# The gate and up products of both feed-forward layers by a seven-product scheme, two of its four weight sums added by an accumulating DMA

## What is computed

```python
def swiglu_ffn(h, w_gate, w_up, w_down):
    return (jax.nn.silu(h @ w_gate) * (h @ w_up)) @ w_down

def reference(...):
    ...
    for i in range(DEPTH):          # DEPTH = 2
        h = rms_norm(h_res, ln_mix[i])
        mix = s5_mixer(...) if i % 2 == 0 else sink_window_attention(...)
        h_res = h_res + mix
        h_res = h_res + swiglu_ffn(rms_norm(h_res, ln_ffn[i]),
                                   ffn_w_gate[i], ffn_w_up[i], ffn_w_down[i])
    return rms_norm(h_res, ln_f)[:, N_META:]
```

## Time and profile before

| | |
|---|---|
| three executions | 1181.73, 1182.28, 1182.97 us; median 1182.28 us |
| span of the profiled execution, first to last instruction | 1177.9 us (no separate time is given for it; the runs are 4.4 us above it) |
| PE busy | 1140.4 us, 97% of the span |
| DVE busy | 553.8 us, 47% |
| ACT busy | 412.4 us, 35% |
| POOL busy | 174.8 us, 15% |
| moved by DMA | 104.63 MB, mean 89 GB/s |

### The profile page before, as it was taken

The page is one execution under the profiler, slowest core; times in us unless marked ns, Lnnn a source line. Parts: engine busy times, 40 slices in busy tenths (PEclk is TensorE's granted clock), DMA queues, the critical chain, the costliest instruction groups (busy, mean ns, idle before and its releaser), DMA issues.

```text
span 1177.9 us, 20443 instructions
## 1 busy us (share of the span) xinstructions
PE 1140.4 (97%) x8362; PEld 1025.8 (87%) x8362; DVE 553.8 (47%) x845; ACT 412.4 (35%) x701; POOL 174.8 (15%) x114
## 2 busy tenths in 40 slices
PE   5799999999999999999999899989999999999998
PEld 5688899999999999999999676678888888888887
DVE  7978444443344333444334355455443434434444
ACT  6823232332222222233323455443322223223332
POOL 4699000011111111100000000001111111110000
PEclk9999899999999999999999999999999999999999
DMA  7164333222323232222323211022333233223332
GB/s 141 24 163 111 87 109 108 72 89 91 98 80 100 78 107 71 76 83 91 98 81 126 72 37 42 32 72 72 108 107 99 79 107 107 75 73 97 98 98 94
DMA packets 119387, 104.63 MB, mean 89 GB/s; under 512 B 21868, under 2 KB 117216, under 8 KB 119008
## 3 DMA queue, kind: packets, MB, share of 16 engines
q1 hardware_dynamic: 110120, 99.85, 27.9%
q10 hardware_dynamic: 9216, 4.06, 1.5%
HBM read 98.11 MB, written 5.24 MB: 88 GB/s over the span
## 4 chain that ended last, share of the span: by engine, by line
PE 90%; DVE 4%; DMA 2%; ACT 1%; POOL 1%; issue 1%; SPq 0%; ACTq 0%; DVEq 0%; POOLq 0%
PE banks L1380 79%; PE banks L1520 1%; PE banks L1457 1%; PE banks L1510 1%; PE banks L1731 1%; PE banks L1734 1%; PE banks L1752 1%; PE banks L1721 1%; PE banks L1458 1%; DMA y_dram<-y_act 1%; PE banks L1746 1%; PE banks L1472 0%; POOL col_mag L499 0%; PE banks L1720 0%; ACTq L719 0%
## 5 line engine op out<-in xcount | busy, mean ns | idle before, releaser
L587 ACT CAST w_high<-raw 128x1024 fp32r<-128x1024 f32 x186 | 195.0, 1049 | 572.1 <-PE banks L1380 572.1
L945 DVE TENSOR_TENSOR w_low<-raw,w_high 128x1024 fp32r<-128x1024 f32 x186 | 228.2, 1228 | 208.3 <-ACT w_high L587 208.3
L1380 PE MATMUL banks<-x_high,w_high 128*128 128x512 f32 (+2 forms) x1184 | 321.0, 324 | 1.0 <-DVE x_low L1173 1.0
L1380 PE MATMUL banks<-x_high,w_low 128*128 128x512 f32 (+2 forms) x1184 | 318.5, 322 | 0.0
L1380 PE MATMUL banks<-x_low,w_high 128*128 128x512 f32 (+2 forms) x1184 | 317.7, 321 | 0.0
L1380 PEld LDWEIGHTS banks<-x_high,w_high 128*128 128x128 f32 x1184 | 198.9, 189 | 19.4 <-issue 2.2
L1380 PEld LDWEIGHTS banks<-x_low,w_high 128*128 128x128 f32 x1184 | 198.9, 188 | 16.1
L1380 PEld LDWEIGHTS banks<-x_high,w_low 128*128 128x128 f32 x1184 | 198.2, 188 | 16.8
L1380 PE MATMUL banks<-a_high,w_high 128*128 128x256 f32 (+2 forms) x533 | 141.2, 318 | 0.0
L1380 PE MATMUL banks<-a_low,w_high 128*128 128x256 f32 (+2 forms) x533 | 141.1, 318 | 0.0
L1380 PE MATMUL banks<-a_high,w_low 128*128 128x256 f32 (+2 forms) x533 | 141.1, 318 | 0.0
(11 more groups left out here) (288 smaller groups left out, 1249.3 us busy)
## 6 DMA issues: line engine op xcount, KB each, us to landing
raw<-in_ffn_w_gate SPq DMA_DIRECT2D x22, 1024.0 KB, 5.3
raw<-in_ffn_w_up SPq DMA_DIRECT2D x22, 1024.0 KB, 5.3
raw<-in_ffn_w_down SPq DMA_DIRECT2D x16, 768.0 KB, 4.4
raw<-in_ffn_w_down SPq DMA_DIRECT2D x16, 640.0 KB, 4.1
raw<-in_attn_w_qkv SPq DMA_DIRECT2D x6, 1024.0 KB, 5.0
k_toep<-k_dram SPq DMA_DIRECT2D x64, 64.0 KB, 2.6
raw<-in_ssm_w_glu_b SPq DMA_DIRECT2D x4, 1024.0 KB, 5.5
raw<-in_ssm_w_glu_a SPq DMA_DIRECT2D x4, 1024.0 KB, 5.8
```

What stands on the lines that cost most here:

```text
L587: nc.scalar.copy(high[:, j], raw[:, slot, :, j * P:(j + 1) * P]).then_inc(w_rounded, 1)
L945: nc.vector.tensor_tensor(low[:, j], raw[:, slot, :, j * P:(j + 1) * P], high[:, j], ALU.subtract).then_inc(w_split, 1)
L1380: ins = nc.tensor.matmul(banks[:, bank + h, b0:b0 + cn], w[:, j, k, :], xx[:, first_k + k, c0 + base:c0 + base + cn], start=start and k == ...
```

## The change

The gate tile and the up tile of 256 columns become one "unit" each. A unit's weights are cut into blocks: input features in even and odd blocks of 128 (4 pairs, `KP`), columns in two halves. The tokens are cut into two halves too (264 or 256). The four quarter outputs, which took eight products of quarters, come from seven products with sums of quarters (the form with 15 additions). Four of the additions are on the weights, four on the input (made once a layer, `x_t`, and kept as slots T1 to T4 of `xs_high`/`xs_low` beside the three plain ones), seven on the outputs.

The weight sums: `raw` has five block columns now. SP loads the even rows into blocks 0 and 1, the odd rows into 3 and 4, and the odd rows' second half once more into block 2 (256 KB). When the three have landed, POOL issues a DMA that adds the even rows from HBM onto blocks 1 and 2 (512 KB, `add_sums`). DVE makes the other two sums, `sum2` and `sum4`. All seven forms of a unit's weights are rounded by ACT and split by DVE.

The outputs: three intermediate sums are copied from PSUM by ACT (`copied_part`), three quarter outputs are added or subtracted by DVE, the fourth is read from its bank. `silu` of both gate blocks is one instruction. The factor `rstd_row` is no longer put on the gated activations by POOL; the results of the down products are multiplied by it on DVE (`scale_down`). The down product is done in three stages, after 4, 8 and 11 pairs of units, over 3, 4 and 4 pairs of feature blocks, each added onto the residual. POOL's descriptor area is 4096 bytes. The loops of ACT and DVE over the feed-forward are written out.

```diff
-DOWN_TILES = ((0, 6), (6, 6), (12, 5), (17, 5))
+KP = KB // 2
+STAGES = ((0, 3), (3, 7), (7, 11))
+UPS = ((0, 4), (4, 8), (8, 11))
+UNITS = 2 * N_UP + N_DOWN * len(STAGES)
+TOK = HALF
+Y_BANK, W_BANK, X_BANK = (0, 4), (1, 5), (2, 6)
+B11, B21, B22, T1, T2, T3, T4 = range(7)
...
+            def load_unit(layer, unit, src):
+                g, kp = UNITS * layer + unit, pairs_of(unit)
...
+                    sp.wait_ge(t_split, forms_before(g - 1))
+                w, blocks = src.rearrange("p (k i) n -> p k i n", i=2), blocks_of(g, kp)
+                for i in range(2):
+                    sp.dma_start(blocks[:, :, 3 * i:3 * i + 2, :].rearrange("p k o c -> p k (o c)"), w[:, :, i, :]).then_inc(unit_loaded[g % 2], 16)
+                if is_up(unit):
+                    sp.dma_start(blocks[:, :, 2, :], w[:, :, 1, P:]).then_inc(unit_loaded[g % 2], 16)
...
-                        nc.gpsimd.tensor_tensor(gate[:, j, a:e], gate[:, j, a:e], rstd_row[:, a:e], ALU.mult).then_inc(gate_scaled, 1)
+            def add_sums(layer, i, w):
...
+                pool.wait_ge(unit_loaded[g % 2], 16 * loads_before(g + 2))
+                nc.gpsimd.dma_start(blocks_of(g, KP)[:, :, 1:3, :].rearrange("p k o c -> p k (o c)"), rows_even,
+                                    accum_op=ALU.add).then_inc(sums_landed[g % 2], 16)
...
+                def gate_unit(i, behind):
+                    g, kp = UNITS * layer + up_unit(i), KP
+                    copy_first(g)
+                    round_column(g + 1, kp)
+                    copy_sum(g)
+                    round_s2(g + 1, kp)
+                    if behind:
+                        round_acts(i - 1)
+                    copy_last(g)
+                    round_sums(g + 1, kp)
...
+                    round_corner(g + 1, kp)
+                    round_s4(g + 1, kp)
...
+            def sum2(g, kp):
+                dve.wait_ge(sums_landed[g % 2], 16 * (ups_before(g) // 2 + 1))
+                if g > 0:
+                    dve.wait_ge(t_split, forms_before(g))
+                    dve.wait_ge(s4_made, ups_before(g))
+                w = blocks_of(g, kp)
+                TT(s24[:, 0, 0:kp], w[:, :, 0, :], w[:, :, 2, :], ALU.add).then_inc(s2_made, 1)
...
+                def gate_unit(i, behind):
...
+                    sum2(g + 1, kp)
+                    sum4(g + 1, kp)
...
+                    first_corner(g, gate_part(n, 0, 0))
...
+                    split_column(g + 1, kp)
+                    if behind:
+                        split_acts(i - 1)
+                    split_s2(g + 1, kp)
+                    last_corner(g, gate_part(n, 1, 1))
...
+                    split_sums(g + 1, kp)
+                    low_corner(g, gate_part(n, 1, 0))
...
+                    TT(gate_part(n, 0, 1), bank_part(Y_BANK[g % 2], n), rstd_part(n, 1), ALU.mult).then_inc(set_free, 1)
...
+                    split_corner(g + 1, kp)
+                    split_s4(g + 1, kp)
...
+            def part(w, i, x, slots, c, bank, n, start=False, need=None):
+                for m, slot in enumerate(slots):
+                    if need is not None:
+                        need(m)
+                    for a, b in ((0, 0), (0, 1), (1, 0)):
+                        ins = nc.tensor.matmul(bank_part(bank, n), w[a][:, m, i, :], x[b][:, slot, c, :],
...
+                ins.then_inc(part_done, 1)
+            def summed_unit(g, ups, downs, parity, x, n, first=False, spread_at=None, mean_at=None, need_b11=None, need_all=None):
...
+                pe.wait_ge(t_split, forms + (4 if first else 1))
+                part(col, 0, x, slots, B11, y, n, start=True, need=need_b11)
+                if spread_at is not None:
+                    spread(spread_at, n)
+                part(col, 1, x, slots, B21, v, n, start=True, need=need_all)
+                pe.wait_ge(t_split, forms + (4 if first else 2))
+                pe.wait_ge(part_copied, 3 * ups + 1)
+                part(w2, 0, x, slots, T2, y, n)
+                if mean_at is not None:
+                    mean(mean_at, n)
+                pe.wait_ge(t_split, forms + (5 if first else 3))
+                part(sums, 0, x, slots, T3, w, n, start=True)
+                pe.wait_ge(part_copied, 3 * ups + 2)
+                part(sums, 1, x, slots, T1, y, n)
+                pe.wait_ge(t_split, forms + (5 if first else 4))
+                pe.wait_ge(part_copied, 3 * ups + 3)
+                part(w2, 1, x, slots, T4, w, n)
+                pe.wait_ge(t_split, forms + 5)
+                pe.wait_ge(c22_made, ups + 1)
+                part(w2, 2, x, slots, B22, y, n)
...
-    nc = _bacc.Bacc("TRN2", target_bir_lowering=False, num_devices=1)
+    nc = _bacc.Bacc("TRN2", target_bir_lowering=False, num_devices=1, dynamic_dma_scratch_size=4096)
```

More of the change, by code:

```diff
@@ L335, in tokens_of @@
             return ap if n == L else ap[:, META:L]
-        def layer_rows(full, short, m, n):
-            return rows(full, m, 0, L) if n == L else rows(short, m, 0, SEQ)
         def cols(ap, n):
@@ L837, in feed_forward @@
                 if layer == 0:
-                    with act.Fori(0, N_DOWN, 1) as i:
-                        down(i, False)
-                else:
-                    with act.Fori(0, N_DOWN - 1, 1) as i:
-                        down(i, False)
-                    for off in range(6):
-                        round_weights(QUAD_DOWN[layer] + 2 * (N_DOWN - 1), 2 + off)
-                    updated(adds0 + KB - 2, KB - 2, n, gain)
-                    for h in range(2):
-                        r_h = half_tokens(h)
-                        act.wait_ge(added, adds0 + KB - 1 + h + 1)
-                        nc.scalar.activation(gate[:, 0, r_h], residual[:, KB - 1, r_h], ACT.Square).then_inc(squared, 1)
@@ L851, in _ @@
-            feed_forward(0, L, N_GLU, KB, 0, "ln_mix1")
+                    for m in range(KB - 2, KB):
+                        normed(m)
+                        squared_of(KB + m, m, n)
+                else:
+                    for q in range(2):
+                        act.wait_ge(last_ready, q + 1)
+                        nc.scalar.activation(last_sq[:, :, q * h:(q + 1) * h], residual[:, KB - 2:, half_tokens(q)],
+                                             ACT.Square).then_inc(squared, 1)
@@ L853, in _ @@
+            feed_forward(0, L, 0)
             for off in range(4):
@@ L1276, in _ @@
-            norm(0, L)
-            feed_forward(0, L, N_GLU, KB, 0, "ln_mix1")
-            norm(1, L)
+                    for m in range(KB - 2, KB):
+                        normed(m)
+                        square_added(KB + m, n)
+                else:
+                    g = UNITS * (layer + 1) - 1
+                    dve.wait_ge(down_added, 2 * KB * (layer + 1))
+                    for q in range(2):
+                        for j in range(2):
+                            dve.wait_ge(part_done, parts_before(g) + 2 * q + j + 1)
+                            last_quarter(g, 4 * (g % 2) + 2 * q + j, j, q, part_added if j == 0 else last_ready)
+                        last_scaled(q)
+                        if q == 1:
+                            last_mean(0)
@@ L1618, in last_mean @@
                     nc.tensor.matmul(banks[:, MEAN_BANKS[h], t:t + 1], sq_sum[:, tokens], ones[:, 0:1], start=True, stop=False)
-                    ins = nc.tensor.matmul(banks[:, MEAN_BANKS[h], t:t + 1], gate[:, 0, tokens], ones[:, 0:1], start=False, stop=True)
+                    for j in range(2):
+                        ins = nc.tensor.matmul(banks[:, MEAN_BANKS[h], t:t + 1], last_sq[:, j, t * P:(t + 1) * P], ones[:, 0:1],
+                                               start=False, stop=j == 1)
                 ins.then_inc(mean_summed, 1)
@@ new lines, in plain_product @@
+            def plain_product(x, weights, slots, it0, bank, n, cut, need):
+                for m, slot in enumerate(slots):
+                    if need:
+                        pe.wait_ge(act_split, 2 * (it0 + m) + 2)
+                    for i in range(2):
+                        for a, b in ((0, 0), (0, 1), (1, 0)):
+                            for h, (c0, cn) in enumerate(cut):
+                                ins = nc.tensor.matmul(banks[:, bank + h, 0:cn], weights[a][:, m, i, :], x[b][:, slot, i, c0:c0 + cn],
+                                                       start=m == 0 and i == 0 and a == b, stop=m == len(slots) - 1 and i == 1 and a == 1)
+                ins.then_inc(part_done, 1)
@@ new lines, in plain_unit @@
+            def plain_unit(g, ups, downs, parity, x, s, layer, n):
+                p0, p1 = STAGES[s]
+                slots, it0 = [p % SLOTS for p in range(p0, p1)], N_UP * layer + p0
+                pe.wait_ge(set_free, g - 1)
+                forms = 5 * ups + 2 * downs
+                cut = ((0, TOK), (TOK, TOK)) if n == L else ((0, SEQ),)
+                for j, weights in enumerate((col, sums)):
+                    pe.wait_ge(t_split, forms + j + 1)
```

(9 more changed lines are left out.)

767 lines of the change are left out of this document (554 added, 213 removed).

## The result

| | before | after |
|---|---|---|
| median of the runs on one chip | 1182.01 us (4 runs) | 1200.31 us (4 runs, 1196.32 to 1201.07) |
| span of the profiled execution | 1177.9 us | 1198.2 us |
| mean granted clock | 0.994 | 0.982 |

The ratio is 1.0164, with a 95% interval of 1.0131 to 1.0196. The forecast was 1164 us and faster. The range held the time, the sign was wrong.

A forecast was written before the change was run, and what follows sets the result against it. PE, busy 97% of the span, was taken as the bound. -49.6 + 0.4 + 1.6 + 19.2 + 3.1 + 3.0 + 0.7 + 2.6 + 0.6 = -18.4 us, from 1182.3 to 1164 us; range 1143 to 1205 us.

The forecast's parts named there:

- 0.2 + 6.3 + 5.5 = 12.0 us: Gate unit's weights: engine wakes, load and accumulate until the sums land, 1.2 us too long; 16 times, +19 us.
- the break-even accumulate: Accumulate time at which the change gains nothing: 6.65 us, with the chain 2.35 us over its 10.8.
- The budget of 10.8: Time from a weight slot's release to the sums' landing that a gate unit allows without waits: 10.8 us.
- its own slope: Cost of each further microsecond of load and accumulate, over 16 gate units: 16 us.
- Stage borders cost nothing: Where down-product stages change: last pair of the first product needed 4.4 us after its start, split 4.0 after part 7.
- stays there if PE's waits stay short: PE's granted clock in the feed-forwards: 1.00, the upper level of 2.4 GHz, held while PE's waits are short.
- the seams' waits: PE waiting for input forms at the feed-forwards' starts: 4.1 us in layer 0 (+3.1), +3.0 us in layer 1.
- the terms of the forecast without it: Forecast for the whole kernel with no waits for load and accumulate: 1144.7 us.
- -49.6 us: PE time removed by fewer matmul columns in the gate and up products: 32.0 us in layer 0, 17.6 in layer 1.
- 8.9 us of work: DVE's work in a gate unit with activations behind it: 8.9 us of the unit's 10.2, so busy sums fit.
- The walk from release to landing: Gate unit's order on DVE and ACT: sums must land 3.45 us into the unit, leaving 10.8 us from slot release.
- The slow accumulate: Rival, chance 0.24: accumulating DMA slow, kernel slower; 1199 us at 7.5 us with the dearer load, 1217 at 9.

The follow-up runs named there:

- the first experiment: Changed kernel with the accumulating DMAs left out, their waits put on the unit's loads; 1153.69 us, ratio 0.9793 to the kernel before.
- the first two experiments: Changed kernel without the accumulating DMAs, 1153.69 us; and with those DMAs kept but writing without adding, 1159.85 us.
- the kernels in which POOL adds: Changed kernel, POOL computing two weight sums, no third load or accumulating DMA: 1162.04 us; also with activations later, filler matmuls, last unit's wait moved: 1149.32 us.
- The fillers: Changed kernel with 32 useless matmuls ahead of the wait for the last input pair in each layer's first unit; 1194.16 us, ratio 1.0123.
- a reordering: Changed kernel with the activations' rounding moved behind ACT's last copy and their split behind DVE's last corner; 1191.36 us, ratio 1.0107.

## Why the prediction was wrong

**The accumulate chain and the stage borders: the steps that failed, by their size.** The prediction put "0.2 + 6.3 + 5.5 = 12.0 us". In the 16 gate units that it priced, the trace has 13.07 us in the mean from the load's issue to `sum2` (12.9 in the median): 6.57 until the last of the three pieces landed, 0.40 until POOL started behind it (0.1 was charged), 6.07 for the accumulate and 0.03 until DVE. So the accumulate was 0.6 us over its 5.5, and load and POOL's start together 0.6 over theirs. With these at 7.0 us the break-even accumulate is 6.1 us, not 6.65; the accumulate itself was inside its bounds (3.7 to 7.5). The budget of 10.8 was read rightly (the slot is released 2.8 us after the unit's end by the walk and in the trace; up units hardly wait). By its own slope the 1.05 us more cost 16.8 us, which gives 1181 us, no change. PE in fact waited 24.3 us in these 16 units, 1.5 in each, against 19.2 and 1.6 for their margins.

The measured price of the whole chain is 43.9 us against the forecast's 19.2. The larger part of what is missing stands where "Stage borders cost nothing" was said: in the first pair of units of each stage PE waited 17.1 us (the longest at 520.7, 2.8 us), and 3.7 of these are left without the accumulate. With 24.3 in the 16 units and 0.9 in up units these 13.4 us make up the 38.5 of the first experiment. Why the border units wait so long was not taken apart further.

**The clock.** "stays there if PE's waits stay short" was taken for granted, and the seams' waits were priced by their length only. They were 4.8 us at layer 0 (forecast 4.1) and 4.0 us at layer 1 (forecast 3.0), with 3.0 us more ahead of layer 1's first matmul. These are 1.0 in the first two experiments and 2.9 and 3.5 in the kernels in which POOL adds; why is open. At each of the two seams PE ran 10.2 us at 1.2 GHz. The fillers took most of that away. By the mean granted clocks, 0.982 of 1198.2 us and 0.994 of 1177.9, the whole span lost 21.6 us of full clock against 7.1; a part of these 14 us more fell on waits and cost nothing. In attention and its projections the changed kernel's execution had 13.6 us at half clock and the kernel before 3.4; that is about 5 us of the +6.4, and not settled, since no edit touches that stretch and the other runs show 3.4 to 13.6 there.

**The last unit.** Its wait for two forms ahead of all products holds PE for 2.5 us (DVE's split of line 1512, above). The prediction did not look at it.

**Without the chain** the kernel stands at 1157.8 us by the first experiment (its forecast was 1163), 13 us above the terms of the forecast without it (1144.7): by that run's trace some 2.3 us more of seam waits, 6.8 of half clock behind them (6.8 us each at half pace), 2.8 at the last unit with 1.7 of half clock. What the stretches at half clock far from the edits add or take from one execution to the next, a few us, stays open.

**The columns: right.** Matmuls of 264 columns start 0.1214 us apart, and units without a wait take 10.20 us in layer 0 and 10.08 in layer 1, half of the forecast's 20.39 and 20.16; -49.6 us is there.

**DVE's list: right in size, wrong in role.** 8.9 us of work were forecast for a gate unit, and it takes 9.1 to 9.5 us from `sum2` to the last split. It was compared with the 10.2 us of matmuls, where it fits. It had to be added to the chain: 13.05 + 9.4 against two units, 20.4. The walk from release to landing gave the same shortage for the changed kernel, since it is the same ring cut open at the deadline, but it made a reordering look worth several times what it was (24 us expected, 6.7 measured).

**The rivals.** The slow accumulate (0.24) had the right sign; its condition, over 6.65 us, was not met. (Its sums leave out the 0.2 us of wakes: they should give 1202 us at 7.5 us and 1220 at 9.) The combination of two terms each about a tenth over was not among the cases: the chain as a whole should have been the uncertain quantity, not the accumulate with the load fixed. That the range held the time is luck: its upper part stood for a slow accumulate, and the time came there by other terms.

**The 4.4 us.** The prediction took them for what a timed run has above its span. In every profiled execution whose own time is on record the difference is 1.8 us; the rest is one execution's difference from the median. The forecast, the median plus a change, does not depend on it.

## What to carry to other kernels

- A slot that is loaded, worked on and loaded again is a ring. Add its whole round (issue, load, every transfer that follows on it, the consumer's list up to the last reader) and compare it with the time of all units between two loads of the slot (here two); that is a floor for the period that no order inside the list moves. But count first how much PE waits where the ring would be shorter: no more than that can be won. Each further transfer put in series with a load lengthens it by its latency, however idle the DMA engines are.
- A wait of some microseconds on PE can cost more than its length, because the matmuls behind it may run at half clock; look at the granted clock behind each seam, and find work for PE there.
- Freeing a buffer sooner starts its next load sooner; look at which transfer it then falls upon.
- The first units behind a change of stage have waits of their own; price them apart from the steady ones.

## What the runs showed of the hardware

- An accumulating DMA of 512 KB from HBM into SBUF in rows of 1 KB lands 6.0 us after its issue, the same without adding 4.2 us. POOL's instruction takes 1.3 us in place of 0.76, a transfer is made of 528 packets in place of 144, and the queue's share of the DMA engines is twice as large. The Trainium skill (Collectives: The Full Stack, The bandwidth ceiling: the fold count and why AG ≠ RS ≠ AR) says of a collective's adding step that it reads two sources over one ring and so moves its data at half the rate. The doubled share, 13.1% against 6.7%, agrees; whether it comes from the second read or from the smaller packets, no run here tells apart. An estimate of 3.2 us for the plain transfer, worked out from the figures of the Trainium skill (DMA: Bandwidth & Descriptors, Anatomy of one DMA), is 1 us under the 4.2 measured.
- In three kernels a unit's load of 1.25 MB was issued between 0.3 us ahead of an accumulate and 0.9 us behind it, five times in all. These five accumulates took 8.4 to 9.8 us; every other one in the traces took at most 7.6, the median 6.0. No experiment moved the two apart.
- The three issues of one unit's load on SP start 0.41 and 0.55 us apart, the third as much as 1.6 us behind the second; in the unit above it is out 2.1 us after the first one's start.
